# The V projection of a two-layer trunk, computed as seven block products for eight with weight sums made a stage earlier

## The reference, cut to what matters

```python
x = x + (y * jax.nn.silu(gate)) @ a_w_out[layer]      # layer 0, D_RNN = 2560 -> 2048
kv = _rmsnorm(x, kv_norm) @ w_kv                      # shared by layer 1
k = kv[..., :D_ATTN]                                  # 2048 columns
v = kv[..., D_ATTN:]                                  # 2048 columns: this product is changed
# layer 1: own q and gate projections, stick-breaking attention over k and v,
# gate, output projection with b_w_out, residual, final RMSNorm
```

## Time and profile before

| what | value |
|---|---|
| median of 3 runs | 1698.17 us (1697.96 to 1698.24) |
| the profiled execution, its own time | 1697.99 us |
| its span, first to last instruction | 1696.3 us |
| PE busy | 1681.1 us, 99% |
| DVE, ACT, POOL busy | 53%, 46%, 14% |
| data moved | 170.87 MB, mean 101 GB/s |
| stage V in the trace | 727.4 to 903.4 us |

### The profile page before, as it was taken

One profiled execution on the slowest core, in us unless ns is written; L12 is line 12 of the kernel. 1 busy time (PEld: TensorE's weight loads), 2 busy tenths in 40 slices (PEclk: granted clock), 3 DMA queues, 4 the chain that ended last, 5 costly groups with the idle time before them and its releaser, 6 DMA issues.

```text
span 1696.3 us, 23428 instructions
## 1 busy us (share of the span) xinstructions
PE 1681.1 (99%) x7839; PEld 1407.6 (83%) x7839; DVE 895.3 (53%) x1600; ACT 778.8 (46%) x1542; POOL 229.1 (14%) x219
## 2 busy tenths in 40 slices
PE   8999999999999999999999999999999999999998
PEld 6888888888888888888888888888888888888888
DVE  5666676666765343442223556464655556463333
ACT  7655566665555232333334544454444535432223
POOL 0121221112112010120000111111111111112100
PEclk9999999999999999999999999999999999999999
DMA  5333333333332222333343322223232232323223
GB/s 183 100 102 97 99 94 98 93 97 95 103 97 98 94 99 93 98 94 120 123 123 120 103 92 85 94 87 99 75 105 88 91 98 76 106 75 115 92 96 134
DMA packets 154269, 170.87 MB, mean 101 GB/s; under 512 B 9992, under 2 KB 135128, under 8 KB 154072
## 3 DMA queue, kind: packets, MB, share of 16 engines
q1 hardware_dynamic: 154200, 170.02, 31.8%
HBM read 161.59 MB, written 8.39 MB: 100 GB/s over the span
## 4 chain that ended last, share of the span: by engine, by line
PE 98%; ACT 1%; DVE 0%; DMA 0%; issue 0%; POOL 0%; SPq 0%; POOLq 0%; DVEq 0%; ACTq 0%
PE ps L398 96%; PE ps L537 1%; PE ps L427 0%; DMA xraw<-in_x 0%; PE ps L582 0%; DVE rbuf L1056 0%; POOL y_lo L1257 0%; ACT w_hi L641 0%; PE ps L434 0%; ACT abuf L729 0%; DVE w_lo L909 0%; DVE tbuf L1052 0%; ACT L729 0%; ACT rbuf L717 0%; ACT tbuf L726 0%
## 5 line engine op out<-in xcount | busy, mean ns | idle before, releaser
L398 PE MATMUL ps<-x_hi,w_hi 128*128 128x512 f32 x1408 | 551.5, 392 | 0.0
L398 PE MATMUL ps<-x_hi,w_lo 128*128 128x512 f32 x1408 | 548.7, 390 | 0.0
L398 PE MATMUL ps<-x_lo,w_hi 128*128 128x512 f32 x1408 | 548.6, 390 | 0.0
L917 DVE SCALAR_TENSOR_TENSOR w_lo<-stage,cT,w_hi 128x256 fp32r<-128x256 f32 x352 | 198.8, 565 | 393.0 <-ACT w_hi L649 384.1
L647 ACT ACTIVATE w_hi<-stage,cT 128x256 fp32r<-128x256 f32 x352 | 178.7, 508 | 375.6 <-PE ps L398 375.5
L398 PEld LDWEIGHTS ps<-x_hi,w_lo 128*128 128x128 f32 x1408 | 264.6, 188 | 55.3
L398 PEld LDWEIGHTS ps<-x_hi,w_hi 128*128 128x128 f32 x1408 | 264.8, 188 | 53.9 <-issue 0.4
L398 PEld LDWEIGHTS ps<-x_lo,w_hi 128*128 128x128 f32 x1408 | 264.7, 188 | 53.6 <-issue 0.2
L909 DVE TENSOR_TENSOR w_lo<-stage,w_hi 128x512 fp32r<-128x512 f32 x160 | 129.1, 808 | 241.6 <-ACT w_hi L641 241.6
L641 ACT ACTIVATE w_hi<-stage 128x512 fp32r<-128x512 f32 x160 | 100.6, 631 | 265.2 <-PE ps L398 264.0
L919 DVE SCALAR_TENSOR_TENSOR w_lo<-stage,cT,w_hi 128x256 fp32r<-128x256 f32 x352 | 180.5, 513 | 0.0
(11 more groups left out here) (164 smaller groups left out, 2035.0 us busy)
## 6 DMA issues: line engine op xcount, KB each, us to landing
stage<-in_a_w_in SPq DMA_DIRECT2D x160, 256.0 KB, 2.7
stage<-in_w_kv SPq DMA_DIRECT2D x128, 256.0 KB, 2.6
stage<-in_b_w_in SPq DMA_DIRECT2D x128, 256.0 KB, 2.6
stage<-in_a_w_out SPq DMA_DIRECT2D x80, 256.0 KB, 2.7
stage<-in_b_w_out SPq DMA_DIRECT2D x64, 256.0 KB, 2.5
v_scratch<-v_f SPq DMA_DIRECT2D x16, 256.0 KB, 3.9
v_lo<-v_scratch SPq DMA_DIRECT2D x8, 512.0 KB, 4.4
out<-x SPq DMA_DIRECT2D x8, 512.0 KB, 3.3
```

What stands on the lines that cost most here:

```text
L398: mm = pe.matmul(dst, a, b, start=start and n == 0, stop=stop and n == 2, skip_group_check=not check)
L917: nc.vector.scalar_tensor_tensor(w_lo[:, slot, 0:256], stage[:, slot, 0:256], cT[:, col:col + 1], f(w_hi[:, slot, 0:256]), ALU.mult, ALU.s ...
```

## The change

V is now computed with the weight columns in VG = 2 groups of 1024. In each, the tokens are split in two halves of 256, the weight rows into even and odd tiles of 128 (VP = 8 pairs of them), and the columns into two halves of 512: a two by two block product, done with seven block products (p1 to p7) for eight. The left operands of p5, p6, p7 and p3 are sums of token blocks (S1 to S4), the right ones of p5, p6, p7 and p4 are sums of weight blocks (T1 to T4). An operand is 128 x 512 weights and is used by 6 matmuls, two token tiles by three. There are 7 x 8 x 2 = 112 of them, for 64 units.

- In the first 4 of stage 1's 5 iterations, every 9 units, SP loads four raw 256 KB blocks of w_kv into b_raw, DVE makes the four sums in five instructions (`block_sum`), and SP stores them to t_scratch (16 rounds).
- In stage 2, POOL makes four token sums of 128 x 256 for each pair of tiles ahead of its two squares' sums. ACT now rounds both tiles before it squares them.
- In stage V the ring has 6 slots (two in memory that y held in stage 2). ACT and DVE make hi and lo of each operand and, spread over the steps, of 32 token sums of 128 x 256. The results of the block products are combined by DVE and scaled by ACT.
- POOL prepares masks for the attention only after the last operand.

The diff, cut to its core (declarations of semaphores, the scaling helpers, v_store and the removed functions are left out; they are printed above or follow the same pattern):

```diff
+B1, B2, B3 = BLOCKS // 2, KD // 4, PAIRS // 2
...
+U3 = U2 + N2 * B2
...
-LINE_GAP = 192
+LINE_GAP = 64
...
+VG, VP = 2, KD // 2
...
+VRING, AHEAD_V = 6, 5
+S1, S2, S3, S4 = range(4)
+STAT_AT, SPREAD_AT = 42, 48
+S2_HI_AT = {2: 4, 3: 5, 4: 7, 5: 9, 6: 11, 7: 13}
+S3_HI_AT = {i: 8 + 2 * i for i in range(VP)}
+S1_HI_AT = {i: 13 + 2 * i for i in range(VP)}
+S4_HI_AT = {i: 30 + 3 * i for i in range(VP)}
...
+T_IN, T_SUM, T_OUT = 16, 3, 24
+def operand(q):
+    g, o = divmod(q, NO)
+    if o < 2 * VP:
+        return g, o // 2, ("p1", "p6")[o % 2]
+    if o < 4 * VP:
+        return g, o // 2 - VP, ("p7", "p5")[o % 2]
+    return g, (o - 4 * VP) // 3, ("p2", "p4", "p3")[(o - 4 * VP) % 3]
+OPERAND = {operand(q): q for q in range(VOPS)}
 LOG1P_TERMS = (1 / 17, 1 / 15, 1 / 13, 1 / 11, 1 / 9, 1 / 7, 1 / 5, 1 / 3)
...
+            gap("below_y", 38 * 1024, mem12)
+            with ExitStack() as mem_y:
...
+            def blocks_in(it, c):
+                if not isinstance(it, int) or 4 * it + c:
+                    sp.wait_ge(t_out, it * 256 + 64 * c)
+                rows = w_kv.rearrange("(n r) c -> n r c", r=4 * P)
+                for n, (odd, half) in enumerate(((0, 0), (0, 1), (1, 1), (1, 0))):
+                    row, col = P * (2 * (c // 2) + odd), D + 1024 * (c % 2) + 512 * half
+                    src = rows[at(it, 1), row:row + P, col:col + 512].rearrange("n r c -> (n r) c")
+                    sp.dma_start(b_raw[:, n, :], src).then_inc(b_in, 16)
+            def sums_out(it, c):
+                sp.wait_ge(t_made, it * 20 + (5 * c + 5))
+                for n, which in ((1, T1), (2, T2), (0, T3), (3, T4)):
+                    dst = t_scratch[which].rearrange("(n r) c -> n r c", r=2 * P)
+                    dst = dst[at(it, 1), P * (c // 2):P * (c // 2) + P, 512 * (c % 2):512 * (c % 2) + 512]
+                    sp.dma_start(dst.rearrange("n r c -> (n r) c"), b_raw[:, n, :]).then_inc(t_out, 16)
+            def block_sums(it, j, first=False, last=False):
+                for c in range(4):
+                    for at_j, step in ((T_OUT, sums_out), (T_IN, blocks_in)):
+                        n, e = divmod(9 * c + at_j, N1)
+                        if e == j and not (first and n) and not (last and not n):
+                            step(it - n if isinstance(it, int) or n == 0 else sp.snap(it - n), c)
             for j in range(RING, N1):
                 load(src1(j // 18, j), j, False, U1 + j)
+                block_sums(0, j, first=True)
+            with sp.Fori(1, B1 - 1) as it:
...
+            def v_store(g):
+                for n, (t, h) in enumerate(V_STORES):
+                    if n < 2:
+                        sp.wait_ge(c11_taken, 2 * g + n + 1)
+                    else:
+                        sp.wait_ge(v_taken, 6 * g + n - 1)
+                    sp.dma_start(v_scratch[:, t, 1024 * g + 512 * h:1024 * g + 512 * h + 512],
+                                 v_f[:, t, 512 * h:512 * h + 512]).then_inc(v_stored, 16)
...
+            def operand_load(q):
+                g, i, name = operand(q)
+                slot = q % VRING
+                if q >= VRING:
+                    sp.wait_ge(op_lo, q - VRING + 1)
+                elif slot < RING:
+                    sp.wait_ge(lo_ready, U3 - RING + slot + 1)
+                else:
+                    sp.wait_ge(w_used, U3)
+                if q == 0:
+                    sp.wait_ge(t_out, 16 * 4 * VP * VG)
...
+                sp.dma_start(v_staged(q), src).then_inc(op_full[slot], 16)
...
                 load(src3(0, j), j, False, U3 + j)
                 if j == V_STORE:
+                    v_store(1)
...
+            def value_product(q):
+                g, i, name = operand(q)
+                if name == "p1":
+                    if g == 0:
+                        pe.wait_ge(x1_lo_ready, 2 * i + 1)
+                    elif i == 0:
+                        pe.wait_ge(c11_taken, 2 * g)
+                if name == "p2" and i == 0:
+                    pe.wait_ge(u2_ready, 2 * g + 2)
+                    pe.wait_ge(x1_lo_ready, KD)
...
+                if name == "p7" and g and i == 0:
+                    pe.wait_ge(c21_ready, 2 * g)
+                if name == "p5" and g and i == 0:
+                    pe.wait_ge(c12_ready, 2 * g)
+                if name == "p4" and i == 0:
+                    pe.wait_ge(u3_ready, 2 * g + 2)
+                if name == "p3" and i == 0:
+                    pe.wait_ge(c22_ready, 2 * g + 2)
+                if name in V_SUM and g == 0:
+                    pe.wait_ge(s_lo_ready[V_SUM[name][0]], i + 1)
+                pe.wait_ge(op_lo, q + 1)
+                hi_w, lo_w = v_weights(q)
+                for t in range(2):
+                    if name in V_SUM:
+                        which, banks = V_SUM[name]
+                        left = s_high(which, i)[:, P * t:P * t + P], s_lo[:, which, i, P * t:P * t + P]
+                    else:
+                        m_hi, m_lo, odd, first, banks = V_LEFT[name]
+                        c = first + P * t
+                        left = m_hi[:, 2 * i + odd, c:c + P], m_lo[:, 2 * i + odd, c:c + P]
+                    mm = product(ps[banks[t]][:, :], left[0], left[1], hi_w, lo_w,
+                                 i == 0 and name in ("p1", "p6", "p7", "p5"), i == VP - 1, check=False)
+                mm.then_inc(op_used, 1)
...
+            for q in range(VOPS):
+                if q == STAT_AT:
+                    token_sums()
+                if q == SPREAD_AT:
+                    spread(2, ps[1])
+                value_product(q)
...
                     if pos == 10 * b + 11:
                         for m in range(2):
                             act.wait_ge(res_step, it * 8 + (4 * b + m + 3))
+                            nc.scalar.copy(x_hi[:, bass.ds(it * 4 + (2 * b + m), 1), :],
+                                           x1[:, m:m + 1, :]).then_inc(x1_hi_ready, 1)
+                        for m in range(2):
                             act.wait_ge(acc_step, it * 4 + (2 * b + m + 1))
                             nc.scalar.activation(sq[:, m, :], x1[:, m, :], ACT.Square).then_inc(sq_ready, 1)
-                            nc.scalar.copy(x_hi[:, bass.ds(it * 4 + (2 * b + m), 1), :],
-                                           x1[:, m:m + 1, :]).then_inc(x1_hi_ready, 1)
...
+            def operand_hi(q):
+                g, i, name = operand(q)
+                dst = v_weights(q)[0]
+                act.wait_ge(op_full[q % VRING], 16 * (q // VRING + 1))
+                if q < RING:
+                    act.wait_ge(w_used, U3 - RING + q + 1)
+                elif q < VRING:
+                    act.wait_ge(w_used, U3)
+                else:
+                    act.wait_ge(op_used, q - VRING + 1)
...
+            def sum_hi(which, i):
+                act.wait_ge(s_step, 4 * i + 4)
+                nc.scalar.copy(s_high(which, i), s_raw[:, which, i, :]).then_inc(s_hi_ready[which], 1)
+            def take_p6(g):
+                act.wait_ge(op_used, NO * g + 2 * VP)
+                act.wait_ge(s_step, 4 * VP)
+                act.wait_ge(sq_ready, KD)
+                for t in range(2):
+                    nc.scalar.copy(u2[:, t, :], ps[t][:, :]).then_inc(p6_taken, 1)
...
+            def value_step(q):
+                operand_hi(q)
+                for which, at in ((S2, S2_HI_AT), (S3, S3_HI_AT), (S1, S1_HI_AT), (S4, S4_HI_AT)):
+                    for i, step in at.items():
+                        if step == q:
+                            sum_hi(which, i)
+                if q == STAT_AT + AHEAD_V + 1:
+                    act.wait_ge(sqrt_in, 2)
+                    nc.scalar.activation(small[:, 1, :], small[:, 1, :], ACT.Sqrt).then_inc(sqrt_out, 1)
+                g, o = divmod(q, NO)
+                if o == 2 * VP + AHEAD_V - 1:
+                    take_p6(g)
+                if g:
+                    if o == 3:
+                        take_c11(g - 1)
+                    if o == 5:
+                        scale_c22(g - 1)
+                    if o == 7:
+                        scale_c21(g - 1)
+                    if o == 9:
+                        scale_c12(g - 1)
...
                 for q in range(N2):
+                    if not last or q + AHEAD < N2:
+                        hi_at(2, N2, U2, it, last, q)
+                    if last and q in (2, 3):
+                        sum_hi(S2, q - 2)
+                    if last and LOOK <= q < LOOK + 4:
+                        value_step(q - LOOK)
                     work2(it, q + LOOK)
+                    if last and q == LOOK + 4:
+                        value_step(4)
+                    if last and q == LOOK + 5:
+                        value_step(5)
+                        value_step(6)
             with act.Fori(0, B2 - 1) as it:
                 body2(it, False)
             body2(B2 - 1, True)
...
+            def block_sum(it, c, n):
```

(121 more changed lines are left out.)

270 lines of the change are left out of this document (166 added, 104 removed).

## The result

Median 1688.26 us of 4 runs (1687.19 to 1688.68) against 1698.11 for the kernel before (1697.96 to 1698.24): a ratio of 0.9941, 95% interval 0.9924 to 0.9958. The forecast was 1680.2 in a range of 1676.2 to 1688.0, so the time lies 8.1 us above the forecast and 0.3 above the range. The profiled execution took 1688.68.

The account below looks back on a forecast made before the run. TensorE (PE), busy 99% of the span with 98% of the chain, was taken as the bound. 1697.99 - 21.8 + 1.3 (handoffs) + 2.5 (start of stage V) = 1680.0, median 0.2 above: 1680.2 us, range 1676.2 to 1688.

Parts of the forecast that it names:

- The matmuls, -21.8: Stage V: 768 matmuls become 672, 96 fewer at 0.2267 us each, -21.8 us; 154.2 us if PE never waits.
- Stage 1, "Hidden" and 0: Stage 1: late weight loads hidden, DVE's sums beside the recurrence just hidden (2.9 of 3.0 us spare); cost 0, bounds 0 and 12 us.
- Its own sign of being wrong: The forecast is wrong if PE waits for w_lo in stage 1 or for a transfer anywhere.
- The rival "stage 1 loses some": Stage 1: PE waits 0.7 to 1.5 us in eight places, giving 1686 to 1692 us; chance 0.14.
- The start of stage V, +2.5 within 0.4 to 5.0: Start of stage V: PE waits 2.5 us as POOL's work lengthens DVE's; 0.4 low end, 5.0 if every POOL instruction collides.
- The handoffs, +1.3: Inside stage V's groups: p4 waits for make_u3 and p3 for make_c22, 0.4 each in group 0, p3 0.45 in group 1.
- The steady pace: Stage V: at 1.36 us an operand, ACT (about 1.0) and DVE (1.1) keep up, with 5.3 us spare; zero cost.
- the norm: Stage V: diagonals are ready 4.2 us after the release and spread wants them at 6.8; zero cost.
- the stores: Stage V: group 0's eight stores delay the next load until 1 to 2 us after its hi could start, within 5.3; zero.
- the transfers of stage V: Stage V: 256 KB each 1.36 us is 193 GB/s, a DMA share of about 0.6; loads have 6.7 us and take 2.6.
- The rival that transfers can't keep up: Stage V: transfers held at 181 GB/s take 162 us, 10 more, giving 1692 us; chance 0.06.
- The rival without any wait at the handoffs and the start: Stage V: neither handoffs nor the start cost anything, giving 1676.4 us; chance 0.12.

Follow-up runs that it names:

- e2: The changed kernel with the rounds' loads and stores but without DVE's five sums, raw blocks being stored; median 1681.54 us, 0.9901 of the kernel before.
- e3: The changed kernel with DVE's sums of all rounds but one load of blocks and no stores; median 1682.17 us, 0.9907 of the kernel before.
- e4: The changed kernel with rounds alternating between two block buffers, whole computation; median 1681.03 us, 0.9897 of the kernel before.
- e10: The changed kernel with two block buffer sets and early sums, late squares, and u3 and C22 made first; 1678.02 us, 0.9882 of the kernel before.

## Why the prediction was wrong

**The matmuls, -21.8: right.** 96 fewer, stage V with its waits taken out is 159.92 - 3.8 - 1.9 = 154.2, the figure forecast, and no other stage changed.

**Stage 1, "Hidden" and 0: this step failed, by 6.1 us.** It priced the round's effects on the weight load behind SP's wait, and DVE's busy time beside the recurrence. Its numbers were good: SP was to wait 3.2 us at `blocks_in`, and it waited from 249.91 to 253.12; the weight load's lateness was hidden, as e2 shows; the sums' places beside POOL were "just hidden", and e3 and e4 lose 0.3 and 0.2 in all of stage 1. What it never priced was the load's own consumer: when the blocks land against when DVE comes to the first sum. The rows of before had enough to raise the question: 2.0 + 3.9 for the stores, as the forecast has it, then 1.5 to the last load's issue and at least 2.6 to its landing, 10.0 us at the least through one buffer. The stores go out behind the load of unit 24, so behind w_lo of unit 20, DVE's step 8; the next first sum stands in step 12, four units of 2.72 later, 10.9 us at most. 10.0 at the least against 10.9 at the most is no cover to count on; measured were 12.6 against 8.5. The forecast named what is queued behind SP's wait, and not what is queued behind DVE's at `b_in`. Its own sign of being wrong, a wait of PE for w_lo in stage 1, is what came.

**The rival "stage 1 loses some" gave 1686 to 1692 and the time is 1688.26, but by another mechanism.** It had the sums meet POOL, 0.7 to 1.5 us in each of eight places. Those meetings do occur at their full length (1.79 and 1.51), and without the loop they cost 0.3 at most. With it, seven of the eight places lose 0.3 each, 2.0 of the 6.1, and the larger part lies at another place, where the rival had nothing. That the time falls into its range is luck. A second buffer is shown to be a cure; whether later sums with one buffer would be one too, no run tried.

**The start of stage V, +2.5 within 0.4 to 5.0: 3.8, a size.** POOL made DVE's instructions longer as said, and the first wait was forecast at 1.2 us and was 1.5. In between I took four meetings of 0.7; there were five, of 0.5 to 1.1. The forecast's low end without POOL, 0.4, measured 0.9.

**The handoffs, +1.3: 1.9, a size.** The waits came where they were forecast (u3's adds in group 0, c22 in both) and p4 of group 1 had a short one too that was forecast as none. The forecast had no price for PE's restart, of which below, 0.1 each.

**The steady pace, the norm, the stores, the transfers of stage V: right, nothing.** DMA share 0.63 and 194 GB/s where 0.6 and 193 were forecast, and no wait of PE between operand 8 and the handoff at 783. The rival that transfers can't keep up (its 1692 should read 1690 by its own terms, 1680.2 + 10) falls with that: e10's stage V has 1.5 us of waits in all. The rival without any wait at the handoffs and the start falls by 5.7 us.

**The sum.** 6.1 + 1.3 (start) + 0.6 (handoffs) + 0.7 - 0.2 = 8.5 us above, against 8.7 by the profiled execution (1688.68 - 1680.0). What stays open: why the one-buffer stage 1 varies from 491.1 to 493.7 between executions; a late store or load would do it, and I didn't separate these.

## What to carry over

Where a change sends data through DRAM and back in one buffer, add up the whole loop (stores' issue, landing, loads' issue, landing) and set it against the time at which the first reader comes to it, and then ask what stands behind that reader in its engine's order. Busy shares, the DMA share and the queue's own wait were all forecast right here and none of them showed the loss; a second buffer, in memory that was free, gave it back. A second look belongs to places where two engines that slow each other are given side work at the moment a stage starts: a later place for the squares cost nothing and gave 2.3 us.
